# A two-layer model on one core: the mask of stick breaking added on TensorE, a shorter slot table for its passes, and a new division of work in the stage of the mixers

## What is computed

```python
proj = xn @ w_in[l]
rq, rk, rv, rg, sq, sk, sv, ga, gb = jnp.split(proj, split_points, axis=-1)
# retention: 8 heads, q and k normed per head and rotated
rq = rope(rmsnorm_2(rq...)); rk = rope(rmsnorm_2(rk...)) * (RET_DK ** -0.5)
ret = group_norm(retention(rq, rk, rv...), ret_group_norm) * jax.nn.silu(rg)
y_a = ret @ w_branch_ret[l]
# stick breaking: 8 heads of 64, q and k normed per head
z = einsum(q, k) * scale
mask = kpos[None, :] < tpos[:, None]
log_stay = jnp.where(mask, jax.nn.log_sigmoid(-z), 0.0)
later = lax.cumsum(log_stay, axis=3, reverse=True) - log_stay
w = jnp.where(mask, jnp.exp(jax.nn.log_sigmoid(z) + later), 0.0)
y_b = (w @ v) @ w_branch_sb[l]
x = x + (jax.nn.sigmoid(ga) * y_a + jax.nn.sigmoid(gb) * y_b) @ w_out[l]
```

## Time and profile before

| | us |
|---|---|
| median of 3 runs (1696.97 to 1697.93) | 1697.71 |
| the profiled execution, its own time | 1696.46 |
| its span, first to last instruction | 1694.7 |
| the stage of the mixers in it, slots 0 to 70 (547.24 to 822.35) | 275.1 |
| of it slots 0 to 31 (547.24 to 677.24) | 130.0 |
| PE busy over the span | 1617.2 |
| DVE, ACT, POOL busy over the span | 1245.4, 751.8, 473.2 |

### The profile page before, as it was taken

How to read it: one execution, slowest core, us unless ns; L and a number is a source line. 1 busy time by engine, 2 the same in 40 slices (tenths; PEclk the granted TensorE clock), 3 DMA queues, 4 the chain that set the end, 5 groups by cost and what they waited for, 6 DMA issues and landing times.

```text
span 1694.7 us, 29073 instructions
## 1 busy us (share of the span) xinstructions
PE 1617.2 (95%) x11502; PEld 1487.2 (88%) x11502; DVE 1245.4 (73%) x2123; ACT 751.8 (44%) x1484; POOL 473.2 (28%) x308
## 2 busy tenths in 40 slices
PE   6999998999999899999898999999999999999999
PEld 6999976889999677889898999999999888888887
DVE  6666687576667676567789999999999655555555
ACT  6544534554455243111234444444444444444443
POOL 1111135211111432333267995333343000000000
PEclk9999999999999899999999999999999999999999
DMA  5556554355565544435434554445444465665654
GB/s 186 179 183 186 182 191 162 113 153 184 186 184 173 165 145 131 138 125 162 142 125 149 165 172 158 155 150 154 147 150 150 162 187 187 188 188 189 191 187 137
DMA packets 77478, 277.87 MB, mean 164 GB/s; under 512 B 8600, under 2 KB 9880, under 8 KB 77344
## 3 DMA queue, kind: packets, MB, share of 16 engines
q1 hardware_dynamic: 77344, 276.02, 51.6%
HBM read 274.94 MB, written 1.05 MB: 163 GB/s over the span
## 4 chain that ended last, share of the span: by engine, by line
PE 70%; DVE 22%; issue 4%; POOL 2%; ACT 2%; DMA 0%; DVEq 0%; SPq 0%; ACTq 0%; POOLq 0%
PE ps L828 70%; DVE WL L345 5%; DVE BIG L1281 4%; DVE XT L1281 2%; DVE OH L1281 1%; DVE HL L1284 1%; DVE BIG L1719 1%; POOL WH L405 1%; DVE SQN L1281 1%; DVE BIG L1714 1%; DVE BIG L1717 1%; DVE BIG L1712 1%; DVE BIG L1715 1%; DVE BIG L1751 1%; DVE BIG L1757 1%
## 5 line engine op out<-in xcount | busy, mean ns | idle before, releaser
L345 DVE TENSOR_TENSOR WL<-RAW,WH 128x1024 fp32r<-128x1024 f32 x455 | 565.9, 1244 | 223.5 <-ACT WH L473 158.3
L828 PE MATMUL ps<-HH,WH 128*128 128x256 f32 x2048 | 592.7, 289 | 17.4 <-DVE HL L1281 4.5
L828 PE MATMUL ps<-HL,WH 128*128 128x256 f32 x2048 | 581.3, 284 | 0.0
L828 PE MATMUL ps<-HH,WL 128*128 128x256 f32 x2048 | 580.8, 284 | 0.0
L473 ACT ACTIVATE WH<-RAW 128x1024 fp32r<-128x1024 f32 x329 | 345.7, 1052 | 204.4 <-PE ps L828 204.4
L828 PEld LDWEIGHTS ps<-HH,WH 128*128 128x128 f32 x2048 | 394.2, 192 | 23.5 <-issue 6.8
L828 PEld LDWEIGHTS ps<-HL,WH 128*128 128x128 f32 x2048 | 394.7, 193 | 1.0 <-issue 1.0
L828 PEld LDWEIGHTS ps<-HH,WL 128*128 128x128 f32 x2048 | 394.6, 193 | 0.0
L405 POOL CAST WH<-RAW 128x1024 fp32r<-128x1024 f32 x181 | 217.7, 1204 | 427.2 <-PE ps L828 424.3
L828 PE MATMUL ps<-WH,GH 128*128 128x512 f32 x512 | 203.0, 397 | 1.8 <-DVE GL L1281 1.8
L828 PE MATMUL ps<-WH,GL 128*128 128x512 f32 x512 | 202.9, 396 | 0.0
(11 more groups left out here) (229 smaller groups left out, 2369.2 us busy)
## 6 DMA issues: line engine op xcount, KB each, us to landing
RAW<-wall SPq DMA_DIRECT2D x510, 512.0 KB, 3.6
B<-rel SPq DMA_DIRECT2D x4, 768.0 KB, 5.5
DEC<-con SPq DMA_DIRECT2D x4, 384.0 KB, 4.2
XT<-xt SPq DMA_DIRECT2D x4, 256.0 KB, 5.3
out<-XT SPq DMA_DIRECT2D x4, 256.0 KB, 2.1
WIN<-con SPq DMA_DIRECT2D x1, 768.0 KB, 8.3
NMASK<-con SPq DMA_DIRECT2D x1, 192.0 KB
PAR<-par SPq DMA_DIRECT2D x1, 190.0 KB, 2.5
```

The source lines that it names most:

```text
L345: ins = eng.tensor_tensor(wl, RAW[:, b % NRAW, :], wh.bitcast(F), ALU.subtract)
L828: return pe.matmul(o, l, r, start=start, stop=stop, skip_group_check=True)
```

## The change

- **Mask.** `stick_scores` adds a matrix MASK (0 where the key is earlier than the query, else -1e30) to the scores on PE, by a matmul with the identity on each 128 x 128 piece of the diagonal. NMASK and its two multiplications on DVE go (`stick_weights` is no more, NS is not multiplied), and the sign moves into TRI and ONES.
- **Passes.** A pass has 7 slots from scores to values' copy, was 9: both `stick_terms` in the third slot after the scores, both `stick_later` in the fourth, both `stick_added` and `stick_exp` in the fifth, `stick_values` in the sixth, `stick_high` and `stick_low` in the seventh. The second pass starts in slot 20, was 21.
- **Blocks.** The order is sqk, sv, rv 0 to 3, rqk 0 to 3, rv 4 to 7, rqk 4 to 7 (was sqk, sv, rqk, rv). Group 6 is rotated in slots 20 and 21 and turned in 22, group 7 rotated in 28 and 29 and turned in 30. Blocks 29 and 30 use the banks from which group 7 is rotated.
- **Norms.** The norm of the input is spread after slot 10, was 5. Retention's root is made in step u = 6, its turn in 6, its spread in 7 (into bank 2, was 3), its norm in 8; each was one slot earlier. ACT squares the centred values out of PSUM (was POOL, out of a copy).
- **Halves.** ACT makes the halves of the stage from block 5 on, except ten (15, 16, 17, 23, 24, 25, 38, 46, 51, 55) that POOL makes.
- Smaller: `GATED_SLOT` is 42, 44, 49, 54 (was 42, 43, 48, 53); the sigmoid of gb is made in two halves, in slots 49 and 53, was both in 52.

The diff, cut:

```diff
-    names.extend(("rqk", k) for k in range(8))
-    for name in ("rv", "rg", "ga", "gb"):
+    for half in range(2):
+        for name in ("rv", "rqk"):
+            names.extend((name, 4 * half + k) for k in range(4))
+    for name in ("rg", "ga", "gb"):
...
+HIGH_MIX = (15, 16, 17, 23, 24, 25, 38, 46, 51, 55)
...
-STICK_SLOT = {12: (0, 1), 21: (2, 3)}
+STICK_SLOT = {12: (0, 1), 20: (2, 3)}
...
+def mixer_bank(i):
+    return (6, 4, 5)[i % 3]
...
             def retention_centred(m):
                 act.wait_ge(s_u3, m + 1)
+                if m >= 2:
+                    act.wait_ge(s_hsum, m - 1)
+                act.activation(NS[:, m % 2, 0:512], bank[3][:, :], ACT.Square).then_inc(s_uq, 1)
                 act.activation(LS[:, m % 2, 0:512], bank[3][:, :], ACT.Copy).then_inc(s_uc, 1)
...
                 for a in range(2):
                     o, r = bank[Z_BANK[m][a]], head_rows(a)
-                    mm(o[:, 0:T], SK[r, m, 0:128], SQ[r, m, :], True, True)
-                    mm(o[:, T:384], SK[r, m, 128:T], SQ[r, m, 128:T], True, True).then_inc(s_z, 1)
+                    mm(o[:, 0:T], SK[r, m, 0:128], SQ[r, m, :], True, False)
+                    mm(o[:, 0:128], IDENT, MASK[:, :], False, True)
+                    mm(o[:, T:384], SK[r, m, 128:T], SQ[r, m, 128:T], True, False)
+                    mm(o[:, T:384], IDENT, MASK[:, :], False, True).then_inc(s_z, 1)
...
-                    if i < 3:
-                        pe.wait_ge(s_evn, 8 if i == 2 else 10)
+                    if i == 0:
+                        pe.wait_ge(s_evn, 10)
+                    elif i < 3:
+                        pe.wait_ge(s_nsq, 14 + i)
+                        pe.wait_ge(s_rr, 4 + 2 * i)
...
-                if n == 5:
-                    norm_spread(4, bank[1])
-                if n in (8, 11, 18, 22):
-                    group_turned({8: 4, 11: 5, 18: 6, 22: 7}[n], MNAT)
+                if n in (8, 11, 22, 30):
+                    group_turned({8: 4, 11: 5, 22: 6, 30: 7}[n], MNAT)
+                if n == 10:
+                    pe.wait_ge(s_nev, 10)
+                    norm_spread(4, bank[0])
...
                 stt(N, Z, 0.0, L, ALU.max, ALU.add).then_inc(s_zn, 1)
-                dve.wait_ge(s_zn, m + 1)
-                n2 = N.rearrange("p (a c) -> p a c", a=2)
-                tt(n2, n2, NMASK[:, :].unsqueeze(1).to_broadcast([128, 2, 384]), ALU.mult).then_inc(s_zm, 1)
                 stt(Z, Z, 0.0, L, ALU.min, ALU.subtract).then_inc(s_zs, 1)
...
                     elif u == 5:
                         value_mean(m)
+                    elif u == 6:
                         value_root(m)
-                    elif u == 6:
+                    elif u == 7:
...
-                    elif u == 7:
+                    elif u == 8:
                         value_normed(m)
...
-    put("nmask", -1.0 * (diff > 0))
+    put("mask", np.where(p[:, None] < p[None, :], 0.0, -1e30))
```

More of the change, by code:

```diff
@@ L236, in build @@
         with ExitStack() as ph:
-            NMASK = sb("NMASK", [128, 384], F, ph)
-            TRI, ONES, CEN = (sb(n, [128, 128], F, ph) for n in ("TRI", "ONES", "CEN"))
+            MASK, TRI, ONES, CEN = (sb(n, [128, 128], F, ph) for n in ("MASK", "TRI", "ONES", "CEN"))
             CS, SN = sb("CS", [128, 2, 64], F, ph), sb("SN", [128, 2, 64], F, ph)
@@ L367, in sync_program @@
                     sp.wait_ge(s_x, 32)
-                    for name, t in (("nmask", NMASK), ("tri", TRI), ("ones", ONES), ("cen", CEN)):
+                    for name, t in (("mask", MASK), ("tri", TRI), ("ones", ONES), ("cen", CEN)):
                         sp.dma_start(t[:, :], con_at(name)).then_inc(d_mid, 16)
@@ L1160, in tensor_program @@
                         pe.wait_ge(s_ev, i - 2)
-                        project(b, bank[4 + i % 3][:, 0:T], SBH, SBL, 4, 512 * g).then_inc(s_blk if g else s_sbm, 1)
+                        project(b, bank[mixer_bank(i)][:, 0:T], SBH, SBL, 4, 512 * g).then_inc(s_blk if g else s_sbm, 1)
                 elif n in (56, 57, 59, 61, 63, 65, 67, 68):
@@ L1167, in tensor_program @@
                     pe.wait_ge(s_ev, i - 2)
-                    block(b, bank[4 + i % 3][:, 0:T], RTH, RTL)
+                    block(b, bank[mixer_bank(i)][:, 0:T], RTH, RTL)
                 elif n < 70:
@@ L1628, in vector_program @@
                     eps_of_x(4)
-                if n in (8, 16, 20):
-                    group_mean({8: 5, 16: 6, 20: 7}[n], MSQ)
-                if n in (16, 17, 20, 21):
-                    rotated(6 + (n >= 20), n % 4)
-                for s in (5, 6):
-                    if n - s in STICK_SLOT:
-                        stick_added(STICK_SLOT[n - s][s - 5])
+                if n in (5, 8, 20, 28):
+                    group_mean({5: 4, 8: 5, 20: 6, 28: 7}[n], MSQ)
+                if n in (7, 10):
+                    g = 4 + n // 10
+                    group_root(g)
+                    group_scaled(g, MNAT, natural_banks(g))
+                if n == 10:
+                    norm_root(4)
+                if n == 11:
+                    norm_taken(4, bank[0])
+                if n in (20, 21, 28, 29):
+                    rotated(6 + (n >= 28), n % 4)
+                for m in STICK_SLOT.get(n - 5, ()):
+                    stick_added(m)
                 for c in (n - 1,):
@@ L1639, in vector_program @@
                         i = c - 28
-                        take(b, (RG, GA, GB)[i // 8][:, i % 8, :], bank[4 + i % 3])
+                        take(b, (RG, GA, GB)[i // 8][:, i % 8, :], bank[mixer_bank(i)])
                     elif 52 <= c < 56:
-                        dve.wait_ge(s_gbs, 2)
+                        dve.wait_ge(s_gbs, 1 if c < 54 else 2)
                         for g in range(2):
```

161 lines of the change are left out of this document (70 added, 91 removed).

## The result

The changed kernel takes 1684.74 us (median of 4 runs, 1684.68 to 1687.23); the kernel before took 1697.34 on the same chip (4 runs, 1695.23 to 1697.93). The ratio is 0.993, its 95% interval 0.9915 to 0.9945: 12.6 us faster, inside the range of the forecast (1673.5 to 1686.5), but 17.4 were forecast.

The account below looks back on a forecast made before the run. PE was taken as the bound, so only its waits, clock and added work count: 13.8 + 8.2 + 5.8 - 3.5 - 6.9 = 17.4 us off 1696.5, plus 1.2 for the median, gives 1680.3; range 1673.5 to 1686.5.

Parts of the forecast that it names:

- low clock: Stage's first part: PE's half-speed stretches behind four long waits go with those waits, 8.2 us gained.
- (a) to (e): PE's five single waits in the stage, on SM, MNAT, NS, SBL and rv's second copy, go: 13.8 us gained.
- retention's four: Retention: PE's turn no longer waits four times 1.45 us for DVE's root, which has a slot more; 5.8 us gained.
- new waits: PE waits anew in slots 8, 10, 29, 30 and in retention (3.2): 6.9 us lost, bounds 0 to 11.
- I take ONES, the same shape: Scores: prices each of 16 mask matmuls like the ONES product, 0.22 us, so 3.5 us lost on PE.
- Slot 29: Block 29 needs bank 4 after group 7's mean and first rotation; PE waits 2.0 us.
- rival 4: ACT becomes the maker all wait for, its halves come late: kernel slower, 1705 us; chance 0.03.
- Halves by ACT, cost 0: Stage: ACT's 13 halves more stay within the blocks' cover, a half may come 3.0 us late; cost 0.
- DVE's eight passes "off the path": DVE loses eight passes of about 0.95 us, which only widens the room for NS and SBL; no gain counted.
- rivals, 1: Clock falls at the new waits of slots 29, 30 and 42, 1.7 us each: 1683.7 for both; chance 0.15.
- Rival 2: The new waits don't come, as DVE is quicker without POOL's casts beside it: 6.9 less, 1673.4; chance 0.15.
- 3 (passes too short): The 7-slot pass is too short, PE waits up to a block per pass, clock falls: 1689.5; chance 0.07.

Follow-up runs that it names:

- e3: Changed kernel with each mask matmul on only the 64 rows of its head's scores, half the mask left out; 1679.05 us, one run.
- e12: Kernel before with only the change's division of the halves (ACT makes them from block 5 on, except ten); 1690.09 us, ratio 0.9964.
- e11: e5 with blocks 29 and 30 in banks that group 7 has not taken, waits moved accordingly; 1674.71 us, ratio 0.9876.
- e9: Changed kernel with retention's root, turn and copy of the decays one slot earlier, as before the change; 1687.92 us, ratio 0.9946.
- e10: Changed kernel with all halves of the stage from block 5 on made by POOL again; 1705.95 us, ratio 1.0059 against the kernel before.
- e6: Changed kernel with the mask as DVE's factor again and no mask matmuls, all else kept; 1676.56 us, ratio 0.9881.
- e1: Changed kernel with a head pair's four masks behind both heads' scores, banks opened twice so part of the result is lost; 1678.77 us.
- e5: Changed kernel with the masks grouped behind both heads' scores, each bank opened once, whole computation done; 1679.56 us, ratio 0.9895.

## Why the prediction was right, and where its sum was not

The sign, the range and the place were right: the stage alone moved, the five waits and the low clock in it went, and PE waits for no rest. By its own steps, in the profiled executions:

| term | forecast | measured |
|---|---|---|
| waits (a) to (e) | -13.8 | -13.8 |
| low clock | -8.2 | -8.2 |
| retention's four | -5.8 | -5.8 |
| a wait on GB and one on WL | not named | -1.0 |
| masks | +3.5 | +11.4 |
| new waits | +6.9 | +5.0 |
| sum | -17.4 | -12.4 (stage: -12.3) |

- **The step that failed is "I take ONES, the same shape".** ONES stands among TRI, which has 128 rows like it; a mask stands between products of 64 rows. The price of the mask itself was right: 1.9 us a pass in e3 against 8 x 0.22 = 1.8. Missing were 15 changes of 0.2 us in each pass, and the scores of two heads that no longer run side by side. The bounds of 3.4 and 4.5 were both taken from runs of one kind, the lower one from scores that themselves start in pairs (719.23 and 719.25); the row that would have bounded it, a matmul right behind one with another number of rows, was not looked for. The sum by the Trainium skill's 81 ns (TensorE: Matmul & The Clock Gate, section Back-to-back issue gap), 2.6 us, was further off still.
- **That the time lies in the range is in part luck.** The masks alone would have put it at 1680.3 + 7.9 = 1688.2, outside. What brought it back has nothing to do with them: new waits 1.9 lower than forecast, two old waits of 1.0 that nobody had named, and a profiled execution that lies at the median (1684.69 for 1684.74), where the forecast added 1.2 for the difference.
- **(a) to (e):** gone as told, but which move took which wait away was not tested one by one; e12 shows that ACT's halves alone take 1.9 us off SM and 0.7 off MNAT. SM left 0.45 in slot 10 (1.0 forecast), slot 8 has none (0.3). PE no longer waits for NS. ACT's last `ln` ends 8.2 us behind the scores (600.24 + 1.77 against 593.79; 8.4 before), and 9.8 behind ACT's first copy of them (592.20), for which the forecast took 9.1. From its timeline:

```profile
600.24 1.77 ACT L672 ACTIVATE LS<-LS,ONEC 128x768 f32<-128x768 f32 x2
```

- **Slot 29:** 2.0 forecast, 1.97 measured, by the cause named (e11). Slot 30's 0.4 did not come.
- **Retention:** 3.2 forecast, 2.6 measured, but the reason given, the slot more for the root, is only part. Halves by ACT alone took the four waits from 1.45 to 0.66, since no POOL half slows the root any more (e12); the slot did the rest (e9: 2.0 us). The forecast's sum also had slips: 4.5 - 4.15 is 0.35 and not 0.45, twice; slot 10's durations give 6.3 - 5.5 = 0.8 and not 1.0; and 44.3 us of ACT fall on 32 blocks, 1.4 each, not on 28. The first two move the forecast by 0.4 us, the last only the weight of rival 4.
- **Halves by ACT, cost 0:** right as a cost, wrong as a weight. The prediction treated it as a cover to be checked; it is what carries the change. Without it the same moves, masks on PE included, lose 9 us against the kernel before (e10).
- **DVE's eight passes "off the path":** nearly, 1.3 us (e6). Taking them away was worth less than the masks cost in any form (3.8 to 11.4).

Of the rivals, 1 is half true: in the changed kernel's profile the clock stays full behind slot 29, in six of the experiments it falls there (e1 to e5, e9). Rival 2 (no new waits) and 3 (passes too short) did not come. Rival 4's worry was turned round: POOL as the maker is what everybody waits for. The Trainium skill has a rule of short idle times (TensorE: Matmul & The Clock Gate, section A second HAM failure mode: psum-queue depth-cycling). It did not bear in the stage for waits of 0.3 to 1.8 us: none of them is followed by a low stretch, except the pair of 1.64 and 0.93 us, 0.4 apart, in slot 42 of e10.

## What to carry to other kernels

When an operation is added to an engine, price it where it will stand: read what its neighbours are, and look in the trace for a pair of the same two kinds side by side, not for a lone one of the same shape. Before moving work from an engine with room to the bound one, ask what the old place costs the path (here 1.3 us) and not how long it is busy (7.6). And measure the parts of a combined change in both orders: one that looks like a mere change of hands can be what makes the others pay.
